# Two kernel parts re-cut in a two-stack transformer kernel: gate columns made stationary, branch blocks paired in PSUM banks, ScalarE's roots spread out

## The reference

```python
x = x + 0.5 * _swiglu(_rmsnorm(x, ffn1_norm[i]), ...)
proj = _rmsnorm(x, mix_norm[i]) @ w_in[i]
q, k, v, z, beta_logit, alpha, hy_in = jnp.split(proj, IN_SPLITS, axis=-1)
o_dn = _deltanet_group(q, k, v, z, beta_logit, alpha, ...)
o_hy = _hyena_group(hy_in, ...)
x = x + jnp.concatenate([o_dn, o_hy], axis=-1) @ w_out[i]
x = x + 0.5 * _swiglu(_rmsnorm(x, ffn2_norm[i]), ...)
```

```python
h = rmsnorm(x, norm_mix_g[l])
proj = jnp.einsum('bsd,de->bse', h, w_in[l])      # attention q k v, retention q k v g,
                                                  # short conv b c x, three blocks of gates
gates = jax.nn.sigmoid(gate_pre + b_gate[l]).reshape(B, S, N_BRANCH, D)
y = (gates[:, :, 0] * jnp.einsum('bse,ed->bsd', o_da, w_branch_da[l])
     + gates[:, :, 1] * jnp.einsum('bse,ed->bsd', o_ret, w_branch_ret[l])
     + gates[:, :, 2] * jnp.einsum('bse,ed->bsd', o_sc, w_branch_sc[l]))
x = x + jnp.einsum('bsd,de->bse', y, w_out[l])
x = x + conv_swiglu(rmsnorm(x, norm_ffn_g[l]))    # w_ffn_in, causal conv of 3, w_ffn_out
```

## Time and profile before

| | |
|---|---|
| time, median of 3 runs | 2173.57 us |
| lowest and highest | 2172.22 and 2174.39 us |
| time of the profiled execution | 2168.07 us |
| its span in the trace | 2166.3 us |
| mean granted TensorE clock | 0.984 of full |
| PE busy | 2067.0 us (95% of the span) |
| ACT, POOL, DVE busy | 1035.9 us, 1490.8 us, 953.2 us |

### The profile page before, as it was taken

How to read it: one execution, slowest core, us unless ns; L and a number is a source line. 1 busy time by engine, 2 the same in 40 slices (tenths; PEclk the granted TensorE clock), 3 DMA queues, 4 the chain that set the end, 5 groups by cost and what they waited for, 6 DMA issues and landing times.

```text
span 2166.3 us, 37228 instructions
## 1 busy us (share of the span) xinstructions
PE 2067.0 (95%) x15887; PEld 1881.3 (87%) x15887; DVE 953.2 (44%) x1659; ACT 1035.9 (48%) x1536; POOL 1490.8 (69%) x656
## 2 busy tenths in 40 slices
PE   6999998889999999999889999999899999989999
PEld 6998768879988998768779988999799889988997
DVE  2560476434213560566434212463577026454760
ACT  5443426355445443425355446446544454556442
POOL 6789335338887789344338887768688967677986
PEclk9999999899999999999899999999999999999999
DMA  6755222115555755222115555444455554445553
GB/s 227 225 176 199 93 95 87 35 59 178 192 182 172 225 175 194 96 85 92 41 59 175 177 193 194 159 152 165 145 177 182 198 166 144 152 156 168 182 181 131
DMA packets 250397, 329.63 MB, mean 152 GB/s; under 512 B 9016, under 2 KB 224954, under 8 KB 249722
## 3 DMA queue, kind: packets, MB, share of 16 engines
q1 hardware_dynamic: 249834, 325.15, 45.1%
q0 software_dynamic: 400, 2.10, 0.2%
HBM read 326.18 MB, written 1.05 MB: 151 GB/s over the span
## 4 chain that ended last, share of the span: by engine, by line
PE 54%; DVE 5%; ACT 3%; issue 1%; POOL 1%; DVEq 0%; ACTq 0%
PE psA L413 11%; PE psA L415 11%; PE psA L414 11%; PE psB L413 5%; PE psB L414 5%; PE psB L415 5%; POOL w_lo L955 1%; PE psA L1746 1%; ACT w_hi L569 1%; PE psB L1769 1%; PE psB L1776 1%; DVE yacc L1548 0%; PE psA L1902 0%; PE psA L1904 0%; PE psB L1892 0%
## 5 line engine op out<-in xcount | busy, mean ns | idle before, releaser
L955 POOL TENSOR_TENSOR w_lo<-raw,w_hi 128x1024 fp32r<-128x1024 f32 x600 | 1456.3, 2443 | 603.7 <-ACT w_hi L569 601.6
L413 PE MATMUL psA<-xT_hi,w_lo 128*128 128x256 f32 x3296 | 948.5, 288 | 32.1 <-DVE xT_lo L1005 15.3
L414 PE MATMUL psA<-xT_lo,w_hi 128*128 128x256 f32 x3296 | 936.2, 284 | 0.0
L415 PE MATMUL psA<-xT_hi,w_hi 128*128 128x256 f32 x3296 | 936.0, 284 | 0.0
L569 ACT ACTIVATE w_hi<-raw 128x1024 fp32r<-128x1024 f32 x600 | 630.4, 1053 | 402.1 <-PE psB L415 247.4
L413 PEld LDWEIGHTS psA<-xT_hi,w_lo 128*128 128x128 f32 x3296 | 635.9, 193 | 44.8 <-issue 22.6
L414 PEld LDWEIGHTS psA<-xT_lo,w_hi 128*128 128x128 f32 x3296 | 636.2, 193 | 2.0 <-issue 1.9
L415 PEld LDWEIGHTS psA<-xT_hi,w_hi 128*128 128x128 f32 x3296 | 636.0, 193 | 0.0
L1101 DVE TENSOR_TENSOR hT_lo<-hfull,hT_hi 128x256 fp32r<-128x256 f32 x132 | 218.8, 1689 | 2.2 <-ACT hT_hi L691 1.3
L414 PE MATMUL psB<-w_lo,hT_hi 128*128 128x512 f32 x528 | 210.2, 398 | 0.0
L413 PE MATMUL psB<-w_hi,hT_lo 128*128 128x512 f32 x528 | 208.0, 394 | 0.4 <-issue 0.4
(11 more groups left out here) (416 smaller groups left out, 2234.3 us busy)
## 6 DMA issues: line engine op xcount, KB each, us to landing
raw<-in_w_in SPq DMA_DIRECT2D x78, 1024.0 KB, 5.1
...
```

The lines of the kernel that those rows point to most:

```text
L413: nc.tensor.matmul(o, a_lo, b_hi, start=start, stop=False, skip_group_check=skip)
L414: nc.tensor.matmul(o, a_hi, b_lo, start=False, stop=False, skip_group_check=skip)
L415: return nc.tensor.matmul(o, a_hi, b_hi, start=False, stop=stop, skip_group_check=skip)
L955: nc.gpsimd.tensor_tensor(split_half(w_lo, n, kind), raw_half(n, kind), split_half(w_hi, n, kind).bitcast(F32), ALU.subtract)\
```

## The change

Four places change. The order of POOL's and SP's instructions stays as it was.

The diff, cut to its core:

```diff
+bank_order = ((2, 3, 0, 1), (0, 1, 2, 3), (0, 1, 2, 3))
...
+        if i == 3:
+            A(stat[:, 46:47], eps, ACT.Ln, bias=eps)
         if i == 4:
             act.wait_ge(root_mm[1].sem, root_mm[1].due(l, 1))
             A(root_mix[:, 0, :], psB[:, 1, 0:L], ACT.Ln, scale=1.0 / D, **bias)
-            A(eps_row[:, :], psB[:, 1, 0:L], ACT.Identity, scale=64 * EPS / D, bias=stat[:, 18 + l:19 + l])
             if l == 0:
                 A(root_old, ss, ACT.Ln, scale=1.0 / D, bias=eps)
             A(root_tok, total, ACT.Ln, scale=1.0 / D, **bias).then_inc(ch.sem, 1)
         if i == 5:
+            A(stat[:, 45:46], eps, ACT.Exp)
+        if i == 6:
             act.wait_ge(ch.sem, ch.step(l))
             A(root_mix[:, 1, :], root_mix[:, 0, :], ACT.Exp, scale=-1.0)
             A(root_mix[:, 0, :], root_mix[:, 0, :], ACT.Exp, scale=-0.5).then_inc(root_out[1].sem, 1)
             if l == 0:
                 A(root_old, root_old, ACT.Exp, scale=-0.5)
             A(root_tok, root_tok, ACT.Exp, scale=-0.5).then_inc(root_cols[1].sem, 1)
+        if i == 7:
+            A(eps_row[:, :], psB[:, 1, 0:L], ACT.Identity, scale=64 * EPS / D, bias=stat[:, 18 + l:19 + l])\
+                .then_inc(root_out[1].sem, 1)
...
-            if i < 6:
+            if i < 8:
                 mixer_root(l, i)
...
+                A(stat[:, 44:45], eps, ACT.Ln, bias=eps)
...
+                A(stat[:, 43:44], eps, ACT.Exp)
+            if i == 12:
                 act.wait_ge(ch.sem, ch.step(l))
                 A(rr2[:, :, :], rr2[:, :, :], ACT.Exp, scale=-0.5).then_inc(s2["a_root"].sem, 1)
                 act.wait_ge(s2["lam_sum"].sem, s2["lam_sum"].due(l, 1))
...
-        for n in range(KC):
-            act.wait_ge(s2["y_sum"].sem, s2["y_sum"].due(l, n + 1))
-            A(yT_hi[:, n, :], yacc[:, n, :], ACT.Copy).then_inc(s2["yb_hi"].sem, 1)
-        for k in range(8):
+        for b in range(4):
+            act.wait_ge(s2["y_sum"].sem, s2["y_sum"].due(l, b + 1))
+            A(yT_hi[:, 2 * b:2 * b + 2, :], psA[:, b, :].rearrange("p (b n) -> p b n", b=2), ACT.Copy)\
+                .then_inc(s2["yb_hi"].sem, 2)
+            if b in (0, 2):
+                round_half(1, l, 58 + b // 2 + AHEAD)
+        for k in range(2, 8):
             round_half(1, l, 58 + k + AHEAD)
...
                 dve.wait_ge(s1["ba_mm"].sem, s1["ba_mm"].due(l, 1))
-                V.tensor_copy(small[:, 304:336], psA[:, 3, 0:32]).then_inc(s1["ba_out"].sem, 1)
-                dve.wait_ge(s1["ba_out"].sem, s1["ba_out"].due(l, 1))
+                V.tensor_copy(ba_row[:, :], psA[0:16, 3, 0:L]).then_inc(s1["ba_out"].sem, 1)
+            if i == 19:
+                dve.wait_ge(s1["ba_mm"].sem, s1["ba_mm"].due(l, 2))
+                V.tensor_copy(small[:, 304:336], psA[:, 3, L:L + 32]).then_inc(s1["ba_out"].sem, 1)
+                dve.wait_ge(s1["ba_out"].sem, s1["ba_out"].due(l, 2))
...
-    def split_y(l, n):
-        dve.wait_ge(s2["yb_hi"].sem, s2["yb_hi"].due(l, n + 1))
-        V.tensor_tensor(yT_lo[:, n, :], yacc[:, n, :], yT_hi[:, n, :].bitcast(F32), ALU.subtract).then_inc(s2["yb_lo"].sem, 1)
+    def split_y(l, b):
+
+        v = slice(2 * b, 2 * b + 2)
+        dve.wait_ge(s2["yb_hi"].sem, s2["yb_hi"].due(l, 2 * b + 2))
+        V.tensor_tensor(yT_lo[:, v, :], psA[:, b, :].rearrange("p (b n) -> p b n", b=2), yT_hi[:, v, :].bitcast(F32),
...
             if i == 8:
+                dve.wait_ge(root_out[1].sem, root_out[1].due(l, 2))
...
+            v = rr2[:, 4:6, :]
             if i == 43:
-                v = rr2[:, 4:6, :]
-                V.scalar_tensor_tensor(v, v, cols[:, 2:3], rg[:, :, :], ALU.mult, ALU.mult).then_inc(ch.sem, 1)
-                dve.wait_ge(ch.sem, ch.step(l))
+                V.scalar_tensor_tensor(v, v, cols[:, 2:3], psA[:, 2, :].rearrange("p (b n) -> p b n", b=2),
+                                       ALU.mult, ALU.mult).then_inc(ch.sem, 1)
+                gated = ch.step(l)
+            if i == 44:
+                dve.wait_ge(ch.sem, gated)
+                V.tensor_tensor(v, v, rg[:, :, :], ALU.mult).then_inc(ch.sem, 1)
+                gated = ch.step(l)
+            if i == 45:
+                dve.wait_ge(ch.sem, gated)
                 dve.wait_ge(s2["rg_sig"].sem, s2["rg_sig"].due(l, 1))
-                V.tensor_tensor(v, v, rgs[:, :, :], ALU.mult).then_inc(ch.sem, 1)
-                dve.wait_ge(ch.sem, ch.step(l))
-                V.tensor_tensor(v, v, psA[:, 2, :].rearrange("p (b n) -> p b n", b=2), ALU.mult).then_inc(s2["or_y"].sem, 1)
+                V.tensor_tensor(v, v, rgs[:, :, :], ALU.mult).then_inc(s2["or_y"].sem, 1)
             if i == 47:
                 dve.wait_ge(s2["o_hi"].sem, s2["o_hi"].due(l, 1))
...
-            for half in range(2):
-                dve.wait_ge(s2["gate_sig"].sem, s2["gate_sig"].due(l, 8 * r + 4 * half + 4))
-                if half == 0:
-                    dve.wait_ge(s2["br_mm"].sem, s2["br_mm"].due(l, r + 1))
+            for n, b in enumerate(bank_order[r]):
+                dve.wait_ge(s2["gate_sig"].sem, s2["gate_sig"].due(l, 8 * r + 2 * b + 2))
+                if n < 3:
+                    dve.wait_ge(s2["br_mm"].sem, s2["br_mm"].due(l, 3 * r + n + 1))
                 else:
                     dve.wait_ge(half_used[1].sem, half_used[1].due(l, (53, 55, 57)[r] + 1))
-                for n in range(4 * half, 4 * half + 4):
-                    ps, v = (psB, psA)[half][:, n % 4, 0:L], gates[:, 8 * r + n, :]
-                    V.tensor_tensor(yacc[:, n, :] if r == 0 else v, v, ps, ALU.mult).then_inc(s2["br"].sem, 1)
+                ps = (psA, psB, psA)[r][:, b, :].rearrange("p (b n) -> p b n", b=2)
+                v, y = gates[:, 8 * r + 2 * b:8 * r + 2 * b + 2, :], yacc[:, 2 * b:2 * b + 2, :]
                 if r == 0:
+                    V.tensor_tensor(y, v, ps, ALU.mult).then_inc(s2["br"].sem, 1)
                     continue
-                for n in range(4 * half, 4 * half + 4):
-                    dve.wait_ge(s2["br"].sem, s2["br"].due(l, 8 * r + n + 1))
-                    ins_ = V.tensor_tensor(yacc[:, n, :], yacc[:, n, :], gates[:, 8 * r + n, :], ALU.add)
-                    if r == 1:
-                        ins_.then_inc(ch.sem, 1)
-                        added = ch.step(l)
-                        if n == 7:
-                            dve.wait_ge(ch.sem, added)
-                        continue
-                    ins_.then_inc(s2["y_sum"].sem, 1)
-                    if n % 4 == 1:
-                        split_y(l, n - 1)
-                    if n % 4 == 3:
-                        split_y(l, n - 2)
-                        split_y(l, n - 1)
-                        split_y(l, n)
+                V.tensor_tensor(ps, v, ps, ALU.mult).then_inc(ch.sem, 1)
+                dve.wait_ge(ch.sem, ch.step(l))
+                if r == 1:
+                    dve.wait_ge(s2["br"].sem, s2["br"].due(l, bank_order[0].index(b) + 1))
+                    V.tensor_tensor(y, y, ps, ALU.add).then_inc(s2["br"].sem, 1)
+                else:
+                    dve.wait_ge(s2["br"].sem, s2["br"].due(l, 4 + n + 1))
+                    V.tensor_tensor(ps, y, ps, ALU.add).then_inc(s2["y_sum"].sem, 1)
+                    if b:
+                        split_y(l, b - 1)
+        split_y(l, 3)
...
+        for kc in range(KC):
+            ins_ = product(psA[0:16, 3, 0:L], wba_hi[:, kc, :], wba_lo[:, kc, :], xT_hi[:, kc, :], xT_lo[:, kc, :],
+                           kc == 0, kc == KC - 1)
+        ins_.then_inc(s1["ba_mm"].sem, 1)
+
+    def turn_gates(l):
+
+        pe.wait_ge(s1["ba_out"].sem, s1["ba_out"].due(l, 1))
         for rb in range(RB):
-            t = slice(rb * P, (rb + 1) * P)
-            for kc in range(KC):
-                ins_ = product(psA[:, 3, 16 * rb:16 * rb + 16], xT_hi[:, kc, t], xT_lo[:, kc, t],
-                               wba_hi[:, kc, :], wba_lo[:, kc, :], kc == 0, kc == KC - 1)
+            ins_ = nc.tensor.transpose(psA[:, 3, L + 16 * rb:L + 16 * rb + 16], ba_row[:, rb * P:(rb + 1) * P], ident[0:16, 0:16])
         ins_.then_inc(s1["ba_mm"].sem, 1)
...
+            if i == 18:
+                turn_gates(l)
...
-        pe.wait_ge(s2["ev_dve"].sem, s2["ev_dve"].due(l, 41))
...
-                for c in range(KC):
-                    if r and i == 0:
-                        pe.wait_ge(s2["br"].sem, s2["br"].due(l, 8 * (r - 1) + c + 1))
-                    o = (psB, psA)[c // 4][:, c % 4, 0:L]
-                    v = slice(c * P, (c + 1) * P)
-                    ins_ = product(o, hi[:, v], lo[:, v], x_hi[:, k, :], x_lo[:, k, :], i == 0, i == n - 1)
-                    if i == n - 1 and c == 3:
+                for m, b in enumerate(bank_order[r]):
+                    if i == 0 and r == 0 and b == 0:
+                        pe.wait_ge(s2["ev_dve"].sem, s2["ev_dve"].due(l, 41))
+                    if i == 0 and r == 2:
```

(21 more changed lines are left out.)

2 lines of the change are left out of this document (1 added, 1 removed).

## The result

The changed kernel takes 2135.06 us (median of 4 runs, 2134.15 to 2140.45) beside 2172.89 us before; the ratio is 0.9835, with a 95% interval of 0.9824 to 0.9847. That is 33 to 38 us less. The profiled execution took 2134.34 us, span 2132.5, against 2168.07 and 2166.3: 33.7 us.

What follows compares the result with a forecast made beforehand. PE, busy 95% of the span, was taken to bound the kernel. Gate columns 10.0, ScalarE 6.0, pass 43 2.2 and branch stage 9.6 sum to 27.8 us: 2173.57 - 27.8 = 2145.8 us, range 2138 to 2158.

Steps and rivals of the forecast that it cites:

- Gate columns: 48 small matmuls per layer become 24 of 256 columns and two transposes, clock not falling: 5.0 us a layer, 10.0 together.
- the loss of clock behind the 48 matmuls: Full-size matmuls behind the old gate columns run at half clock: 2.5 us lost in layer 2, 1.9 estimated in layer 1.
- The rival on the clock at the new form: Clock falls at the new gate columns too: 5.8 us less gain, 2151.6 us; chance 0.15.
- DVE's copy and the transposes: At the gate columns, per layer: 0.2 us for two transposes and 0.3 us waiting for DVE's copy of pass 17.
- ScalarE: Start of stack-2 mixer: PE's two waits, 1.26 and 1.7 us, go with table loads and Exp moved; 6.0 us in all.
- Pass 43: DVE's three operations spread over passes, removing PE's wait for a gate bank: 1.1 us a layer, 2.2 in all.
- Branch stage: From the branches' first matmul to `into_x`: 24.8 us instead of 29.44 and 28.65, start wait of 0.52 gone; 9.6 us together.
- the two allowances of 0.2 us for latency: Branch-stage end: 0.2 us added to bank 0 being ready (21.1 us), 0.2 after DVE's five operations (24.8 us).
- `into_x` itself is unchanged: Matmuls after the branch stage were to take as long as before, so no gain was counted there.
- From profile to median: 27.8 us, read from a profiled execution 5.5 us under the median, was subtracted from the median 2173.57 us, giving 2145.8.
- The rival "slower": Mixer scores: newly held-up DVE operations cost up to 2.1 us each; 17 more give 2181.5 us; chance 0.04.
- The better case: Branch end less tightly bound or clock loss regained: 3.4 + 0.4 more and some 2 in clock, 2140.0 us; chance 0.09.

Runs made afterwards that it cites:

- e4: Kernel before, its 48 gate matmuls of 128x16 kept but 12 after each of halves 16 to 19, DVE's copy moved to pass 20: 2157.67 beside 2171.82 us.
- e7: The whole change without its gate columns (the old 48 matmuls of 128x16 kept): 2153.51 us.
- e5: The whole change against the kernel before, measured again: 2139.01 beside 2174.28 us, ratio 0.9844.
- e1: Only the gate columns of the change, against the kernel before: 2159.54 beside 2171.82 us, ratio 0.9941.
- e9: The changed kernel with its 24 gate matmuls of 16x256 issued twice in a row, 48 in all: 2142.04 us.
- run 100: Not a run's label: in "one run 100% busy", run means the 48 old gate matmuls issued in a row, as in the kernel before, 2172.89 us.

## Why the prediction was right or wrong

Over all the experiments the kernel before has a mean of 2172.5 us (54 executions, 2165.9 to 2176.7, mean clock 0.983) and the whole change, with the first result, 2136.7 (16, 2134.2 to 2140.5, mean clock 0.9885): 35.7 us. The forecast had 27.8. The mechanisms of all four places were as predicted; what failed is the size of two terms above all, the gate columns (some 4 us short) and the branch stage (1.8).

- **Gate columns: 10.0 forecast, about 14 found.** The step that failed is the loss of clock behind the 48 matmuls, "2.5 us" and "1.9 us". For the execution that it was read from it was right: 25.73 + 25.67 - 2 x 20.6 = 10.2 us. But its second layer was a mild one: of five traces of the old form, three have 27.3 us from the gates to the squares and not 25.67. The means of the two layers are 25.73 and 26.35, together 52.08, against 2 x 20.6: 10.9. The rest, 1.7 us a layer (standard error 0.5), lies in the stretches behind, and the sum had no term for it. Most of it is clock: the mean loss there is 12.5 us a layer with the old form and 10.6 with the new. The wait of PE for DVE shown at e4 is also 0.2 to 0.35 us shorter. 10.9 + 3.3 = 14.2; e7 against e5 gives 14.5, and e1 12.8 (10.0 to 15.6). Why the falls behind become fewer is not shown: their moments move with everything ahead of them.
- The rival on the clock at the new form is wrong in 18 of 18 stretches: e4 and e9 show PE 100% busy with clock 1.00, the old form in one run 100% busy with 0.50. The Trainium skill (TensorE: Matmul & The Clock Gate, Part 1: The HAM clock gate) explains the clock by how busy PE has been, which was the rival's ground. These rows disagree, and the measurement decides.
- **DVE's copy and the transposes: 0.5 us a layer forecast, 0.46 found.** The full matmuls around them start 0.58 us apart (334.24 and 334.82), where 0.12 is the rule. Right.
- **ScalarE: 6.0 forecast, 6.9 found.** Right in mechanism; the term was taken from the idle column and not from the distance between the starts.
- **Pass 43: 2.2 forecast, 2.45 found.** Right, again but for the idle column.
- **Branch stage: 9.6 forecast, 11.4 found.** The mechanism was right and three sizes were off. The stage ended at 24.38 and not 24.8 us: DVE's first multiply began 20.9 us into it (1500.87 - 1479.98) and not 21.1, and from there to w_out's first matmul it took 3.5 us and not 3.7. No run shows the two allowances of 0.2 us for latency by themselves; together the two ends came 0.4 us sooner than the sum with them. The start came 0.7 and not 0.52 us sooner. And "`into_x` itself is unchanged" was wrong: w_out's halves took 22.48 us and not 22.82.
- **From profile to median.** The difference was read from a profiled execution 5.5 us below the median and was taken from the median. The two profiled executions differ by 33.7 us: 10.2 at the gate columns, 2.4 behind them, 20.8 in stack 2 and 0.3 elsewhere. The means of many executions differ by 35.7 us, since most of those before lose more at the clock than that one. The first result's 37.8 us between medians is 2 more than that, which is chance.
- The rival "slower", more held-up operations on DVE in the scores, left no mark in the trace: PE's starts there moved as a block (1420.11 to 1403.73 and 1464.30 to 1447.90, 16.4 us both).
- The better case, 2140.0, was the nearest rival. It put its extra gain at the branch end and in the clock there; 1.8 us of it came, and the larger part of what was missing came from the clock in stack 1, which no rival had.
- The range failed by 3 us on its lower side. It went 7.8 us below the forecast, 2 of them for the clock, while the executions of the kernel before alone spread over 10.8 us, mostly with the clock.
